# A staging place more, moved loads and moved operand splits in a hybrid gMLP and band-attention step on one core

## What is computed

```python
h = x @ w_in                                   # 1024 -> u_a, v_a, z_a, q, k, v_b, z_b, 512 columns each
u_a = gelu(u_a); v_a = layernorm(gelu(v_a), ln_v_g, ln_v_b)
a = u_a * (tril(w_sgu) @ v_a + b_sgu)          # mixed within chunks of 128 frames, 4 groups
p = softmax(q @ k.T / 8 + rel_bias)            # own chunk of 64 and the 8 before it, 8 heads
b = p @ v_b
y = concat([a * silu(z_a), b * silu(z_b)])
out = layernorm(ALPHA * x + y @ w_out, ln_g, ln_b)
```

## Time and profile before

| | us |
|---|---|
| median of three runs | 1014.32 |
| the three runs | 1012.17, 1014.32, 1014.38 |
| the profiled execution | 1012.61 |
| its span, first to last instruction | 1010.5 |
| PE busy | 994.1 |
| DVE busy | 662.1 |
| ACT busy | 505.1 |
| POOL busy | 284.5 |

### The profile page before, as it was taken

The page is one execution under the profiler, slowest core; times in us unless marked ns, Lnnn a source line. Parts: engine busy times, 40 slices in busy tenths (PEclk is TensorE's granted clock), DMA queues, the critical chain, the costliest instruction groups (busy, mean ns, idle before and its releaser), DMA issues.

```text
span 1010.5 us, 19272 instructions
## 1 busy us (share of the span) xinstructions
PE 994.1 (98%) x7460; PEld 858.8 (85%) x7460; DVE 662.1 (66%) x1262; ACT 505.1 (50%) x994; POOL 284.5 (28%) x253
## 2 busy tenths in 40 slices
PE   8999999999999999999999999999999999999997
PEld 6888887788888899999999977778888888888885
DVE  4776876757667766365565514977777777776765
ACT  5455634444445543333443415766666666666630
POOL 2457554324221042422322000022222222222200
PEclk9999999999999999999999999999999999999999
DMA  6557353466746433335554576664444343333222
GB/s 228 161 167 234 103 169 112 122 176 167 212 149 218 143 98 104 95 90 161 152 156 118 163 251 229 243 215 157 150 144 138 138 139 127 116 118 134 78 81 83
DMA packets 122857, 152.65 MB, mean 151 GB/s; under 512 B 13176, under 2 KB 75792, under 8 KB 122768
## 3 DMA queue, kind: packets, MB, share of 16 engines
q1 hardware_dynamic: 107792, 124.16, 38.1%
q10 hardware_dynamic: 14976, 27.27, 9.0%
HBM read 106.29 MB, written 48.26 MB: 153 GB/s over the span
## 4 chain that ended last, share of the span: by engine, by line
PE 87%; DMA 4%; DVE 3%; issue 2%; ACT 2%; POOL 1%; SPq 1%; ACTq 0%; DVEq 0%; POOLq 0%
PE s_ps L1847 21%; PE oo_ps L2036 17%; PE pt_ps L1847 10%; PE s_ps L1759 7%; PE oo_ps L1998 6%; PE s_ps L1927 5%; PE oo_ps L1847 5%; PE pt_ps L1969 3%; PE pt_ps L1759 2%; PE s_ps L2036 2%; PE s_ps L1777 2%; PE oo_ps L1777 2%; PE s_ps L1956 1%; PE oo_ps L1812 1%; DMA wp_raw<-w_tok 1%
## 5 line engine op out<-in xcount | busy, mean ns | idle before, releaser
L1847 PE MATMUL s_ps<-xo_h,wf 128*128 128x288 f32 (+1 forms) x960 | 232.7, 326 | 2.2 <-issue 1.3
L1847 PEld LDWEIGHTS s_ps<-xo_h,wf 128*128 128x128 f32 x960 | 163.5, 188 | 15.5 <-issue 1.8
L1847 PE MATMUL s_ps<-xo_l,wf 128*128 128x288 f32 (+1 forms) x480 | 156.5, 326 | 0.0
L1591 DVE CUSTOM_DVE_ANT_1 prob<-s_ps,bias 128x640 f32<-128x640 f32 (+1 forms) x112 | 85.7, 803 | 58.9 <-PE s_ps L1927 58.9
L1266 ACT ACTIVATE prob<-prob,low 128x640 f32<-128x640 f32 (+3 forms) x128 | 97.4, 762 | 47.5 <-DVE low L1591 47.5
L1847 PE MATMUL pt_ps<-xo_h,wf 128*128 128x288 f32 (+1 forms) x480 | 119.6, 327 | 0.6 <-DVE cs L1417 0.6
L1372 DVE TENSOR_TENSOR wf<-s,wf 128x512 fp32r<-128x512 f32 x60 | 53.0, 884 | 79.9 <-ACT wf L1066 79.7
L2036 PE MATMUL oo_ps<-wo_h,yh 128*128 128x512 f32 x248 | 101.0, 407 | 0.0
L2036 PE MATMUL oo_ps<-wo_l,yh 128*128 128x512 f32 x248 | 97.4, 393 | 0.0
L2036 PE MATMUL oo_ps<-wo_h,yl 128*128 128x512 f32 x248 | 97.3, 392 | 0.0
L960 POOL TENSOR_TENSOR s<-a,a 128x512 f32<-128x512 f32 x20 | 26.6, 1330 | 245.8 <-DMA a<-w_pair 239.3
(11 more groups left out here) (186 smaller groups left out, 2064.8 us busy)
## 6 DMA issues: line engine op xcount, KB each, us to landing
a<-w_pair ACTq DMA_DIRECT2D x80, 256.0 KB, 2.9
xt_f<-x_tiles SPq DMA_DIRECT2D x44, 256.0 KB, 3.1
r<-x SPq DMA_DIRECT2D x17, 512.0 KB, 3.6
s_k<-st SPq DMA_DIRECT2D x32, 256.0 KB, 2.9
s_q<-st SPq DMA_DIRECT2D x32, 256.0 KB, 2.8
q<-s_q SPq DMA_DIRECT2D x16, 512.0 KB, 3.9
k<-s_k SPq DMA_DIRECT2D x16, 512.0 KB, 5.6
y_out<-r SPq DMA_DIRECT2D x15, 512.0 KB, 2.7
```

The source lines that it names most:

```text
L1591: nc.vector.tensor_tensor_reduce(out=out, in0=src, in1=b, scale=1.0, scalar=MASKED, op0=ALU.add, op1=ALU.min, accum_out=low[:, s:s + 1]).t ...
L1847: made = nc.tensor.matmul(out, wf[:, p, side, kc, :], xx[pas][p][:, kc, c * n:(c + 1) * n], start=kc == 0 and a == 0 and p in (0, 1, 3, 5) ...
```

## The change

It has seven parts.

- v's tiles from 8 on are staged in places 0, 1, 2, 3 in turns instead of 2 and 3. SP's wait ahead of the first stream's values goes to place 0, where tile 16 now stands.
- x's tile 16 gets places 6 and 7 in the region of the weight blocks (which are done by then) and semaphores of its own, and is asked right behind tile 14 instead of in cycle 2.
- The output's weight pieces are split sooner: ACT's 0 and 1 ahead of the second unit's exponents of cycle 2, 2 and 3 around the turned copy of cycle 3 instead of ahead of all of it; DVE's 0 and 1 in cycle 2, 2 and 3 in cycle 3, y's low part ahead of a weight piece.
- Block a22 (j = 3) is asked at step 2, right behind a21, instead of at step 3.
- SP's copy into `s_skew` moves from step 3 to step 6 of a pair.
- The block sum t4 (`sum_xb(5)`) moves from between shared sums to the end of DVE's work between the passes.
- The streams' row sums are made from w_sgu's first 16 rows and columns (16 rows, 64 columns) instead of the 128 by 512 of `wts`; DVE reads them eight times over by a zero stride.

```diff
@@ stores()
-            staged(event, [2 + event[1] % 2], 1)
+            staged(event, [event[1] % 4 if event[1] >= V_MID else 2 + event[1] % 2], 1)
@@ places and semaphores of x tiles
 def xt_place(kind, t, h):
+    if (kind, t) == ("v", TILES - 1):
+        return 6 + h
...
+def xt_signal(kind, t):
+    return 2 if (kind, t) == ("v", TILES - 1) else t % 2
...
-WO_IN = {V_CYCLES - 2: [(), (0,)], V_CYCLES - 1: [(1,), (2, 3)], V_CYCLES: [(4, 5), (6, 7)]}
+WO_IN = {V_CYCLES - 2: [(), (0, 1)], V_CYCLES - 1: [(2,), (3,)], V_CYCLES: [(4, 5), (6, 7)]}
...
-        xt_at = [u_at, u_at + 4096, copy_at, copy_at + 4096, 6 * x_slot + 4096, 6 * x_slot + 8192]
+        xt_at = [u_at, u_at + 4096, copy_at, copy_at + 4096, 6 * x_slot + 4096, 6 * x_slot + 8192,
+                 ring_at + 32768, ring_at + 36864]
@@ SP
-                        if pas == 0 and p == 3 and m < HEADS:
+                        if pas == 0 and p == 6 and m < HEADS:
                             sp.wait_ge(rel_stored, 32)
                             sp.dma_start(s_skew[m, :, 0:REL], ...)
...
                 if t == V_SPLIT - 1:
-                    for h in range(2):
-                        load_xt("v", V_SPLIT + 2, h)
+                    for t_x in (V_SPLIT + 2, TILES - 1):
+                        for h in range(2):
+                            load_xt("v", t_x, h)
...
-                        if V_EARLY + cycle + 1 < TILES:
+                        if V_EARLY + cycle + 1 < TILES - 1:
                             load_xt("v", V_EARLY + cycle + 1, h)
...
-                    sp.wait_ge(st_stored[2], 16 * STORES[2])
+                    sp.wait_ge(st_stored[0], 16 * STORES[0])
@@ ACT, pairs
-                    if p in (1, 2, 3) and m + 1 < (NP * (pas + 1) if p == 1 else ALL_PAIRS):
-                        act.wait_ge(w_ready, BUILT["op", m, {1: 3, 2: 4, 3: 5}[p]])
-                        if p == 1:
-                            act.wait_ge(w_summed, 4 * m + 4)
-                        load_block(m + 1, p)
+                    for j in {1: (1,), 2: (2, 3)}.get(p, ()):
+                        if m + 1 < (NP * (pas + 1) if j == 1 else ALL_PAIRS):
+                            act.wait_ge(w_ready, BUILT["op", m, {1: 3, 2: 4, 3: 5}[j]])
+                            if j == 1:
+                                act.wait_ge(w_summed, 4 * m + 4)
+                            load_block(m + 1, j)
@@ ACT, cycles
                 copy_turned(2 * cycle - 2)
-                if cycle == V_CYCLES - 1:
-                    for j in (2, 3):
-                        high_wo(j)
...
+                if cycle == V_CYCLES - 1:
+                    high_wo(2)
                 copy_turned(2 * cycle - 1)
+                if cycle == V_CYCLES - 1:
+                    high_wo(3)
...
+                if cycle == V_CYCLES - 2:
+                    for j in (0, 1):
+                        high_wo(j)
...
                 for h in range(2):
                     exponent(2 * cycle + 1, h)
-                if cycle == V_CYCLES - 2:
-                    for j in (0, 1):
-                        high_wo(j)
@@ DVE
                     add_shared(5)
-                    sum_xb(5)
                     add_shared(6)
...
                     for p in FIRST_EARLY[1][4:]:
                         w_low_part(("op", NP, p))
+                    sum_xb(5)
...
+                for n in range(TILES):
+                    if START[n] - 1 == cycle:
+                        y_low_part(n)
                 if cycle in WO_IN:
                     for j in WO_IN[cycle][0]:
                         low_wo(j)
-                for n in range(TILES):
-                    if START[n] - 1 == cycle:
-                        y_low_part(n)
@@ PE, mix(0); DVE reads row_ps[1] with [[0, SB], [1, SN]]
-                    for row, held in zip(row_ps, (wt, wts)):
-                        nc.tensor.matmul(row[:], st[3][:, 0:P], held[:].rearrange("p g t -> p (g t)"), ...)
+                    nc.tensor.matmul(row_ps[0][:], st[3][:, 0:P], wt[:].rearrange("p g t -> p (g t)"), ...)
+                    nc.tensor.matmul(row_ps[1][:, 0:GRP * SN].rearrange("p (g n) -> p g n", g=GRP), st[3][0:SN, 0:P],
+                                     wt[0:SN, :, 0:SN], ...)
```

More of the change, by code:

```diff
@@ L234, in xt_place @@
     return 4 + h if kind == "v" and t > V_SPLIT else h
+def xt_signal(kind, t):
+    return 2 if (kind, t) == ("v", TILES - 1) else t % 2
 def xt_loads_before(kind, t):
-    return sum(e[1] % 2 == t % 2 for e in XT_TILES[:XT_TILES.index((kind, t))])
+    return sum(xt_signal(*e) == xt_signal(kind, t) for e in XT_TILES[:XT_TILES.index((kind, t))])
 def xt_user_before(kind, t, h):
@@ L481, in hybrid_stream_step @@
         warm_ready = sem("warm_ready")
-        xt_loaded = [[sem(f"xt_loaded{b}_{h}") for h in range(2)] for b in range(2)]
+        xt_loaded = [[sem(f"xt_loaded{b}_{h}") for h in range(2)] for b in range(3)]
         q_part = sem("q_part")
@@ L630, in load_xt @@
                 sp.dma_start(xt_f[xt_place(kind, t, h)][:],
-                             x_tiles[t, :, HK * h:HK * h + HK, :]).then_inc(xt_loaded[t % 2][h], 16)
+                             x_tiles[t, :, HK * h:HK * h + HK, :]).then_inc(xt_loaded[xt_signal(kind, t)][h], 16)
             def load_xo(kc):
@@ L1069, in xt_high_part @@
                 b = xt_place(kind, t, h)
-                act.wait_ge(xt_loaded[t % 2][h], 16 * (xt_loads_before(kind, t) + 1))
+                act.wait_ge(xt_loaded[xt_signal(kind, t)][h], 16 * (xt_loads_before(kind, t) + 1))
                 nc.scalar.activation(xt_h[b][:], xt_f[b][:], ACT.Copy).then_inc(xt_high, 1)
@@ L1507, in _ @@
                     for g in range(GRP):
-                        add = bs[:, g, 0:SN]
+                        add, row = bs[:, g, 0:SN], row_ps[1][:, g * SN:(g + 1) * SN]
                         nc.vector.scalar_tensor_tensor(out=mix_bs[:, g, :].rearrange("p (b n) -> p b n", n=SN),
-                                                       in0=row_ps[1][:, g * P:(g + 1) * P].rearrange("p (b n) -> p b n", n=SN),
+                                                       in0=bass.AP(row.tensor, row.offset, [row.ap[0], [0, SB], [1, SN]]),
                                                        scalar=v_cols[:, GRP + g:GRP + g + 1],
@@ L1802, in mix @@
                     pe.wait_ge(const_ready, 6)
-                    for row, held in zip(row_ps, (wt, wts)):
-                        nc.tensor.matmul(row[:], st[3][:, 0:P], held[:].rearrange("p g t -> p (g t)"),
-                                         start=True, stop=True).then_inc(row_sums, 1)
+                    nc.tensor.matmul(row_ps[0][:], st[3][:, 0:P], wt[:].rearrange("p g t -> p (g t)"),
+                                     start=True, stop=True).then_inc(row_sums, 1)
+                    nc.tensor.matmul(row_ps[1][:, 0:GRP * SN].rearrange("p (g n) -> p g n", g=GRP), st[3][0:SN, 0:P],
+                                     wt[0:SN, :, 0:SN], start=True, stop=True).then_inc(row_sums, 1)
                 pe.wait_ge(vn_ready, t + 1)
```

## The result

The changed kernel takes 1006.5 us, the median of six runs (1004.49 to 1007.23), against 1013.45 of the kernel before (six runs, 1012.17 to 1014.92). The ratio is 0.992, 95% interval 0.991 to 0.994: 7 us faster. On a second chip it was 0.994 (0.992 to 0.996), 1007.16 against 1013.21. The forecast was 1004.6, with a range from 1002.0 to 1009.5.

What follows compares the result with a forecast made beforehand. PE was busy 994.1 of 1010.5 us, leaving only idle time and slow stretches: 0.35 + 1.5 + 1.41 + 1.12 + 1.03 + 1.04 + 0.83 + 1.5 = 8.8 off 1012.61 or 1014.32 gave 1003.8 or 1005.5; forecast 1004.6, range 1002.0 to 1009.5.

Steps and rivals of the forecast that it cites:

- seven stalls: PE standing still in pairs 2 and 3, pass 1's start, v tiles 12 and 16, units 5 and 8: 7.2 us.
- second and third rivals: Second: middle stage's end stays tight, clock falls, 1008.0, chance 0.18. Third: other waits leave next to nothing, 1012 to 1015, 0.07.
- first rival: Pass 0: the VectorE and GpSimd lock moves with POOL's earlier sums, stalls stay; gain 7.3, 1006.1 us, chance 0.12.
- Row sums, 0.35: First part: smaller row-sum passes let PE go on sooner, 0.35 us, bounds 0 and 0.7; two small passes take 0.1.
- s_skew and a22, 1.5 with 1.8 as the upper bound: Pairs 2 and 3: a22 lands sooner, POOL's sums start earlier, both stalls shrink; 1.5 us, bounds 0 and 1.8.
- less is queued on DVE ahead of that time: Pass 0: argument that POOL's sums, moved to about 147.2, would meet less DVE work than the first rival says.
- t4, 1.41: Start of pass 1: with the block sum later, the first product's low part is ready at about 352.6; 1.41 us won.
- Staging, 1.12: v's tile 12: with four staging places PE no longer waits for the staging copy behind tile 8's store; 1.12 us.
- x's last tile 1.03, output weights 1.04 + 0.83: Middle stage's end: earlier load ends tile 16's stall; sooner weight splits end those at unit 5's weighing and unit 8's scores.
- Clock, 1.5: Behind the middle stage's last three stalls: without them the granted clock stays up; 1.5 us, bounds 1.08 and 1.68.
- The new wait at step 2: ACT waits for DVE's low part of operand 5 before copying sum 2; claimed hidden under PE's product, no cost.
- fourth rival: Middle pairs: ACT's new wait at step 2 ends late and delays PE's product 4; slower, 1017.5 us, chance 0.05.

Runs made afterwards that it cites:

- experiment 1: The changed kernel with block a22 asked at step 3 again, the s_skew copy left at step 6; 1006.3 us, ratio to the kernel before 0.994.
- experiment 5: The changed kernel with the output weights split in the old order, as in the kernel before; 1007.03 us.
- experiment 6: The changed kernel with x's last tile at its old place and asked in cycle 2: 1010.33 us with the old weight order, 1010.43 with the new.

## Why the prediction was right, and where it wasn't

**The sign, the size and the place** were right: six of seven stalls went, each by the part of the change named for it or, for two, by another (below), and the clock held (1.00 from 594 to 660). No run undid the row sums alone; their part is read from the two traces. POOL's sums for pair 2 began at 147.50, "about 147" as forecast, partly by luck: a22 was asked 1.0 us sooner than in the kernel before (143.68) and took 3.7 us to land where 2.5 had been assumed. The second and third rivals have fallen: the end of the middle stage never waited with x's tile in time. The median came 1.9 us above the forecast: the aimed stretches gave 9.3 us, and pair 1 (0.3 to 1.2), pair 16 (0 to 1.2) and the weighing (0 to 0.7) took 0.3 to 3.1 of it back. With that the 1006.5 lies nearer to the first rival's 1006.1 than to the forecast.

- *Row sums, 0.35:* the two sets and the eight mixing products took 2.52 us ahead of the next tile's product before and 2.22 after (22.19 to 24.41). 0.3. The two small passes took 0.36 (23.14 to 23.50), not 0.1.
- *s_skew and a22, 1.5 with 1.8 as the upper bound:* pairs 2 and 3 gave all 1.8 in most executions and 1.3 in the profiled one. But the step "less is queued on DVE ahead of that time" failed for pair 1, which takes 0.3 to 1.2 back, and, if the early a22 is what turns the two issues there, for pair 16, 0 to 1.2. I had walked through the queue behind the sums and not through the three instructions ahead of the sum of product 6. The first rival was half right: the lock moved, to another place than the old stalls.
- *t4, 1.41:* 1.4. It rests on a cover that I didn't name, the store of v's tile that DVE waits for. That held where x's block took 7.8 us to land and the store behind it 5.1 (experiment 1) and failed at 8.3 and 6.8 (experiment 5).
- *Staging, 1.12:* the one execution without it lost 0.3 at that place; the bound below it should have been 0, as the store and PE arrive within a microsecond of each other.
- *x's last tile 1.03, output weights 1.04 + 0.83:* the sum, 2.9 us, was right (2.7 in experiment 6); the share wasn't. The step that failed is that the copy and the bias sums would stay late by themselves. Once the tile is in time both queues empty ahead of them, and the weights' order gave nothing that could be measured.
- *Clock, 1.5:* right where it falls: 8.25 and 8.27 against 6.71 us, of which the 24 output matmuls are 1.1 (6.75 and 6.81 against 5.65 to 5.68) and the scores of unit 8 the rest. But of three traces with the same three stalls it fell in two, so it is worth less on the mean; how much is open.
- *The new wait at step 2* never showed: the low part was ready 1.9 us ahead of ACT's copy in pair 1 (143.65 against 145.58). The fourth rival has fallen.
- *The base of the sum*, between 1012.61 and 1014.32, was met by the median of six, 1013.45. But the rows are those of one profiled execution, 1012.61, which had, with one other, the shortest first part of all 14 traces, 108.98. Others took up to 111.5 there, in code that differs only in the row sums. The kernel before has one trace only, so what its other executions lost at the start is open.

## What to carry to other kernels

Take stalls that follow one another within ten microseconds, as these three did, for one until shown otherwise: find the late transfer at their head, mend it alone, and read again before paying for the rest. When an engine that shares a lock is made to start sooner, walk through what the other engine has queued ahead of the next result that is waited for, not only through what was late before, and put the awaited result ahead of the work that the lock can stretch. And compare stages over several traces: between the two executions of the changed kernel the first part, pairs 0 and 1, and pairs 16 to 19 moved by 0.7 to 1.5 us with no edit at all, as much as most of the seven parts are worth.

## What the runs showed of the hardware

With two issues 0.1 to 0.3 us apart, on the queues of two engines, a 32 KB store landed 2.7 to 2.9 us after its issue when it was the first and 4.8 to 5.5 when a 256 KB load was. The clock at the start came in three ways with the same instructions: full from 4.2 to 5.5 us on (first part 109.0 to 109.4), full and then one stretch of 3.41 us at half (109.8 to 111.3), or matmuls at half the rate up to 9.6 to 13.3 us (109.4 to 111.5). Within the second way the spread goes with PE's waits: up to 1.1 us ahead of the second product of x and up to 0.65 at 30. Both traces with 12 idle products were of the first kind, of the twelve with 8 only two. That the products are the cause is likely and not shown: in one of the two PE still idled 1.35 us ahead of x, as with 8.
